# Attention work between the high and the low products of a wide unit

## The reference, cut to what matters

```python
def first_block(x, ...):
    for i in range(2):
        hn = rms_norm(h, mix_norm[i])
        h = h + (mixer_a(hn, ...) if i == 0 else mixer_b(hn, ...))
        h = h + conv_ffn(rms_norm(h, ffn_norm[i]), ...)
    return rms_norm(h, final_norm)

def mixer_b(h, w_qkv, w_o, rel_bias):          # 3 groups (dilation 1, 4, 16) of 8 heads of 128
    qkv = (h @ w_qkv).reshape(b, s, 3, 3, 8, 128)
    # windowed attention with a bias in each group, then a softmax over the groups
    return y @ w_o

def hybrid_layer(x, ...):                      # 4 mixers of 4 heads
    p = split_columns(rms_norm_2(x, pre_g) @ w_in + b_in)
    # stick-breaking attention, native sparse attention (with a compression of the keys
    # and values by a small network), forgetting attention, latent attention
    mix = concatenate([o_sb * silu(g0), o_nsa * silu(g1), o_fox * silu(g2), o_mla * silu(g3)])
    return x + rms_norm_2(mix @ w_out, post_g)
```

## Time and profile before

| | |
|---|---|
| time, median of 3 runs | 3341.31 us (3338.09 to 3342.93) |
| the profiled execution | 3341.5 us |
| its span, first to last instruction | 3339.3 us |
| TensorE matmuls busy | 3286.9 us, 98% |
| VectorE busy | 2019.1 us, 60% |
| ScalarE busy | 1628.0 us, 49% |
| DMA | 615.54 MB, mean 184 GB/s |

### The profile page before, as it was taken

The page is one execution under the profiler, slowest core; times in us unless marked ns, Lnnn a source line. Parts: engine busy times, 40 slices in busy tenths (PEclk is TensorE's granted clock), DMA queues, the critical chain, the costliest instruction groups (busy, mean ns, idle before and its releaser), DMA issues. The chain is left out here.

```text
span 3339.3 us, 43206 instructions
## 1 busy us (share of the span) xinstructions
PE 3286.9 (98%) x18176; PEld 2854.2 (85%) x18176; DVE 2019.1 (60%) x2448; ACT 1628.0 (49%) x1875; POOL 0.2 (0%) x4
## 2 busy tenths in 40 slices
PE   8999999999999999999999999999999999999998
PEld 7768888888888999998888888888898987898986
DVE  6765774774665555555676576476664654664654
ACT  5554553553444444443554354355554754464743
POOL 0000000000000000000000000000000000000000
PEclk9999999999999999999999999999999999999999
DMA  6525556556556555555555555555754546654545
GB/s 229 176 89 178 189 196 213 190 191 218 189 202 195 180 186 177 183 178 187 177 189 190 195 189 191 193 189 189 249 168 136 159 160 227 219 174 135 166 153 177
DMA packets 499225, 615.54 MB, mean 184 GB/s; under 512 B 21765, under 2 KB 383391, under 8 KB 498008
## 3 DMA queue, kind: packets, MB, share of 16 engines
q1 hardware_dynamic: 495576, 606.49, 54.7%
q10 hardware_dynamic: 3456, 6.29, 0.6%
HBM read 606.39 MB, written 12.63 MB: 185 GB/s over the span
## 5 line engine op out<-in xcount | busy, mean ns | idle before, releaser
L242 DVE TENSOR_TENSOR low<-raw,high 128x2048 fp32r<-128x2048 f32 (+3 forms) x564 | 1242.4, 2204 | 889.4 <-ACT high L234 885.0
L234 ACT ACTIVATE high<-raw 128x2048 fp32r<-128x2048 f32 (+3 forms) x564 | 1041.0, 1847 | 1258.4 <-PE bank L280 607.7
L270 PE MATMUL bank<-h,high 128*128 128x512 f32 x4672 | 1124.5, 393 | 3.0 <-PEq L1658 1.0
L270 PEld LDWEIGHTS bank<-h,high 128*128 128x128 f32 x4672 | 859.8, 188 | 178.2 <-issue 9.2
L280 PEld LDWEIGHTS bank<-h,low 128*128 128x128 f32 x4672 | 599.0, 191 | 22.8
L280 PE MATMUL bank<-h,low 128*128 128x256 f32 x4672 | 606.0, 283 | 0.0
L259 PE MATMUL bank<-high,y_high 128*128 128x512 f32 x1208 | 472.2, 391 | 4.0 <-DVE hy_tmp L2688 2.3
L261 PE MATMUL bank<-high,y_low 128*128 128x512 f32 x1208 | 470.3, 389 | 0.0
L260 PE MATMUL bank<-low,y_high 128*128 128x512 f32 x1208 | 470.2, 389 | 0.0
L259 PE MATMUL bank<-high,h 128*128 128x256 f32 (+4 forms) x1112 | 362.2, 326 | 1.9 <-PEq L1045 1.0
L261 PE MATMUL bank<-high,h 128*128 128x256 f32 (+4 forms) x1112 | 354.8, 319 | 0.0
(11 more groups left out here) (271 smaller groups left out, 1882.2 us busy)
## 6 DMA issues: line engine op xcount, KB each, us to landing
raw<-in_w_up SPq DMA_DIRECT2D x176, 1024.0 KB, 5.0
raw<-in_w_down SPq DMA_DIRECT2D x88, 1024.0 KB, 5.1
raw<-in_w_in SPq DMA_DIRECT2D x84, 1024.0 KB, 4.9
raw<-in_b_w_qkv SPq DMA_DIRECT2D x72, 1024.0 KB, 4.9
raw<-in_w_out SPq DMA_DIRECT2D x32, 1024.0 KB, 5.0
raw<-in_a_w_qkv SPq DMA_DIRECT2D x24, 1024.0 KB, 5.1
raw<-in_b_w_o SPq DMA_DIRECT2D x24, 1024.0 KB, 5.0
raw<-in_a_w_o SPq DMA_DIRECT2D x16, 1024.0 KB, 5.0
```

Source lines behind the costliest of these rows:

```text
L234: act.activation(c.high[u % SPLIT][:, 0:n], c.raw[u % RAW][:, 0:n], ACT.Copy).then_inc(c.w_high, 1)
L242: dve.tensor_tensor(c.low[u % RAW][:, 0:n], c.raw[u % RAW][:, 0:n], c.high[u % SPLIT][:, 0:n].bitcast(F32), ALU.subtract).then_inc(c.w_low, 1)
L270: pe.matmul(banks[:, i, :], wh[:, k, i * P:(i + 1) * P], c.h[:, k0 + k, :, :].rearrange("p a n -> p (a n)"), start=k0 + k == 0, stop=False ...
```

## The change

The attention work of a step with a wide unit is called between `wide_high` and `wide_low`. In steps with another unit it still stands before the unit's products, behind the wait for free banks and, in mixer B, behind the same two lines of bookkeeping. In output steps nothing changes. In the hybrid layers the three calls are put into one method, `pe_attend`.

```diff
@@ MixerB.tensor @@
             self.pe_roots(pe, s)
-            self.pe_heads(pe, s)
             if s < B_STEPS:
                 self.pe_project(pe, s)
             else:
+                self.pe_heads(pe, s)
                 self.pe_out(pe, s)
@@ Hybrid.tensor @@
             self.enter.enter_pe(pe, s)
-            self.pe_heads(pe, s)
-            self.pe_jobs(pe, s)
-            self.pe_compress(pe, s)
             if s < O0:
                 self.pe_project(pe, s)
             else:
+                self.pe_attend(pe, s)
                 self.pe_out(pe, s - O0)
+
+    def pe_attend(self, pe, s):
+
+        self.pe_heads(pe, s)
+        self.pe_jobs(pe, s)
+        self.pe_compress(pe, s)
```

## The result

The changed kernel takes 3350.79 us, the median of 10 runs (3349.5 to 3352.87), and the kernel before 3342.66 us, the median of 10 (3338.09 to 3343.99). The ratio is 1.0026, with a 95% interval of 1.0019 to 1.0034. So the change costs 8.1 us. That is about 0.25%, a little more than the 0.2% that the prediction took as the limit of what can be told, and the interval is clear of 1. The forecast was 3347.3, in a range of 3341.0 to 3351.5. The time is 3.5 us above it and 0.7 us inside the range: 1.4 us of this is the baseline, which ten runs put at 3342.66 and not at 3341.31, and 2.1 us is the size of the change, 8.1 for 6.0. The profile says why.

A forecast was written before the change was run, and what follows sets the result against it. TensorE, busy 98% of the span, was taken to bound the kernel by its stream and standstills. Two layers of 0.93 + 0.70 + 1.24 give 5.7 us, with 0.3 for blocks 6.0; 3341.3 + 6.0 = 3347.3 us, range 3341.0 to 3351.5.

The forecast's parts named there:

- step 18: Hybrid layers, steps 17 to 18: TensorE waits for ScalarE's hidden row behind late exponentials, 0.93 us a layer.
- step 66: Hybrid layers, steps 65 to 66: VectorE's late low part delays the last unit's sums; TensorE waits 1.24 us more a layer.
- step 48: Hybrid layers, steps 45 to 48: ScalarE's late queue delays the copy TensorE waits for, 0.70 us a layer.
- signs of being wrong: Low products of wide steps start late, TensorE waits in steps 19 to 25, or blocks behind high products cost other than 0.79.
- step 30: Hybrid layers, steps 29 to 30: ScalarE's copy comes just in time, 0 lost, upper bound 0.3 us a layer.
- mixer B: Steps 18k+3 to 18k+5: 2.6 us are spare before TensorE turns VectorE's weights, so 0 lost.
- the blocks' own: All 62 moved attention blocks: 0 to 0.01 us each from their new neighbourhood, taken as 0.3 us in all.
- slower: Outcome class for the whole kernel: slower than before by more than 0.2%, chance 0.42.
- within 0.2%: Outcome class for the whole kernel: time within 0.2% of the kernel before, chance 0.54.
- the stalls are taken up: Rival, hybrid layers: one or none of the three stalls remains, 3341.5 to 3345 us, chance 17 in 100.
- the backlog spreads: Rival: ScalarE falls behind where room shrinks, making copies late at each of eleven crossings; 13.6 us, 3355; chance 17 in 100.
- Blocks do get cheaper: Rival: blocks behind 512-column products gain up to 7.4 us, giving 3333.9, or 3339.6 with the stalls; chance 6 in 100.

The follow-up runs named there:

- the one with the early hidden row: Changed kernel with ScalarE making the compression's hidden row ahead of the exponentials in step 17: 3348.96 us, repeated 3349.38 us, against 3342.79 for the kernel before.
- step 65 alone: Kernel before with the attention work moved only in step 65 of each hybrid layer: 3347.42 us against 3343.17, ratio 1.0011.
- mixer B alone: Kernel before with the move made only in mixer B, hybrid layers as before: 3343.5 us against 3343.17, ratio 0.9998.
- 17 alone: Kernel before with the attention work moved only in step 17 of each hybrid layer: 3343.15 us against 3343.17, ratio 1.0001.
- 45 alone: Kernel before with the attention work moved only in step 45 of each hybrid layer: 3343.09 us against 3342.79, ratio 1.0002.
- all but the last: Changed kernel with steps 17, 29, 45 and 65 of each hybrid layer left unmoved: 3345.24 us against 3343.17 for the kernel before, ratio 1.0005.
- the late low part: Changed kernel with VectorE making unit 67's low part in step 66 behind the eviction, not ending step 65: 3345.47 us against 3342.79 for the kernel before.
- the three repairs: Changed kernel with the hidden row early, VectorE's low part late and step 45 unmoved: 3342.83 us against 3342.79 for the kernel before, ratio 1.0004.
- the exchanged units: First two output units of each hybrid layer in exchanged order: 3339.1 us on the kernel before, 3342.97 on the changed one, both against 3342.79.

## Why the prediction was right, and where it was off

**The main claim held.** The change gives TensorE next to nothing, and costs a standstill in each hybrid layer where a moved block is followed by one that is not moved. The three places, the engine that is late and the operation that waits are those of the prediction, and each place is shown with a kernel that moves it alone. Taking away what makes it late removes it at step 18 and all but 0.07 us of it at step 66. At step 48 the stall comes and goes with the move in step 45, and that it runs through ScalarE's queue is read from the rows. None of the signs of being wrong showed: steps 19 to 25 are as long as before within 0.05 us, and the blocks still take 0.79.

**The terms**, forecast and by the trace, for one layer: step 18 0.93 and 1.05; step 48 0.70 and 0.78; step 66 1.24 and 1.25, the wait in front of the output product 2.4 and 2.40; step 30 0, with an upper bound of 0.3, and 0.09; mixer B 0 and 0.00; the blocks' own +0.3 in all, and -0.7, small but of the other sign (between -0.28 and -0.33 a layer in each of the eight profiles of kernels that move most of the blocks). The chains traced are right within 0.12 us. Of the 0.12 at step 18, some 0.11 is the release. I gave it 0.04 us, and L2452 starts 0.15 us after the end of L2621 (2952.37 + 0.18 to 2952.70). Step 30's 0.09 is the same thing. These are ScalarE's copy and the product behind it, after.

```profile
3017.25 0.48 ACT L2590 ACTIVATE hy_prob_t<-bank 128x384 f32<-128x384 f32 x1
...
3017.88 0.38 PE L2363 MATMUL bank<-ident,hy_prob 128*15 128x128 f32 x2
```

Step 29 ends 7.95 us later here than before, and 3017.25 less 7.95 is 3009.30, the copy's start as forecast. L2363 starts 0.15 us after its end. At step 48 that distance is 0.05 (3144.69 + 0.47 to 3145.21), and 0.06 of the 0.08 lies at the start of the chain: ScalarE's copy starts 0.59 us after the moved transposes (3133.99 to 3134.58), for which I had 0.53.

**The term that was missing** is what a longer standstill does to the granted clock. The sum 2 x (0.93 + 0.70 + 1.24) prices the new wait at step 66 as 1.24 us. In the runs a stretch at half clock follows it in many executions, and costs 1.5 to 1.6 us more each time. Five profiles have the wait of 2.40 us (the changed kernel twice, the one with the early hidden row twice, step 65 alone). In their ten layers the clock fell in seven. In the seven profiles with a wait of 1.15 to 1.22 us (before itself, mixer B alone, 17 alone, 45 alone, all but the last, the late low part, the three repairs), fourteen layers, it fell in none, and neither did it in the four layers with no wait. Six of these eighteen layers do have step 65 moved, those of the late low part, the three repairs and the exchanged units, so the move alone is not the cause. With 7 in 10 the changed kernel should be 6.3 - 0.7 + 2 x 0.7 x 1.6 = 7.8 us slower. Its two medians say 8.1 and 7.3. That the fall at this place follows from the longer wait is shown by these kernels. What decides between two executions of one program is not.

Nor is the length of the wait all of it. The same fourteen profiles have two other long waits, in code that no kernel changes. At step 11 of the first hybrid layer it is 1.92 to 2.36 us, and a stretch at half clock follows in all fourteen. In front of a product 207 us from the start it is 1.70 us, with three waits of 0.75 us in the 8 us ahead of it, and there the clock is low in seven of the fourteen. Behind the single wait of 1.71 us that the kernel with all but the last steps has in step 29 it stayed at 1.00 in both layers.

That the time came out inside the range owes something to luck. The range reached to 3351.5 for the sake of a backlog that did not happen, and the fall of the clock, which it did not allow for, used that room up to 0.7 us. By the prediction's own classes the result is "slower", to which it gave 0.42, and not "within 0.2%", to which it gave 0.54.

The Trainium skill ("TensorE: Matmul & The Clock Gate", section Part 1: The HAM clock gate) says of the gate's release at a kernel's start that it varies from run to run with where the work happens to lie against the gate's own timekeeping. No run here shows that timekeeping, nor that it decides the falls here. The two layers of one profile, one with a fall and one without behind the same 2.40 us, would fit it.

**The rivals of the prediction.** That the stalls are taken up did not happen, since all three remained. That the backlog spreads did not happen either: steps 29 to 30 had just the room they needed, 0.09 us short, and mixer B had its 2.6 us. Blocks do get cheaper, but by 0.7 us in all and not by 7.4. L2621 starts 1.30 us after the start of its table load (2951.07 to 2952.37), and step 18 is 1.05 us longer. The Trainium skill ("ScalarE: Activation LUTs", section What ACT_TABLE_LOAD costs) gives a further drain of about 1.38 us for each switch of tables. An estimate with it is 1.05 + 1.38 = 2.4 us for step 18, and the trace does not agree with it.

**What the times alone can tell.** The trace puts 2.1 us on the kernel with step 17 alone, 1.5 on that with 45 alone and 3.8 on that with all but the last steps, and none of the three ratios is clear of 1. The verdict on such an edit comes from the distance of two starts in the trace, here the same in both layers within 0.02 us at steps 18, 29 and 48.

## What to carry to other kernels

When a block of work is moved inside a step, ask first where a moved block is followed by an unmoved one. Inside a run of moved blocks every distance is kept and nothing over 0.06 us happened here, and the price is at the crossings, one queue at a time. A wait of TensorE that is already over a microsecond should not be lengthened even where the sum looks small, since behind the 2.40 us of this one the granted clock fell in seven of ten cases and cost more than the wait's growth. Look through the profile before for waits of that length: what the granted clock does behind them belongs in the forecast. Where such a wait is for a bank of PSUM, let the next unit that writes other banks go first, which took away all of it here (1.41 us a layer in the kernel before).

## What the runs showed of the hardware that was not expected

The granted clock can fall to half behind a standstill of 2.40 us (7 of 10) or of 1.92 to 2.36 us at another place (14 of 14), with no fall at 1.15 to 1.22 us (0 of 14). Whether it falls differs between two layers of one execution and between two executions of one program. In the seven cases at step 66 the slow stretch began between 0.2 us before the first product behind the wait and 1.5 us after it, and lasted 3.4 us. It makes products of 512 columns start 0.43 us apart and not 0.23. Its price is 1.6 us (7.19 against 5.58 us for one unit), and 1.5 where it began before the first product.

A product that waits for ScalarE can start 0.15 us after ScalarE's end, as L2452 and L2363 do, or 0.05 us, as L2382 does. The rows do not tell which property makes the difference.
